# A hybrid trunk layer on one core: the state's decay applied as the state is taken, low-rank products in pairs, the inverse's blocks turned by VectorE, and the modulation blocks whole in the projection phase

## What is computed

```python
sh1, sc1, g1, sh2, sc2, g2 = split(silu(cond) @ ada_w + ada_b, 6)        # ada_w: 1024 x 6144
h = rms_norm(x) * (1 + sc1) + sh1
z = h @ w_in                                                             # 2816 columns
# half of the mixer: RWKV-7, two directions, 8 heads of 64, every step of time:
sa = state @ (-kk_t)
state = state * w_t + sa * b_t + v_t * k_t                               # w_t, b_t from low-rank products
y_t = state @ r_t
# other half: GLU, depthwise convolution of width 31, LayerNorm, swish
x = x + g1 * (concat(y_rwkv * gate, y_conv) @ w_out)
x = x + g2 * moe(rms_norm(x) * (1 + sc2) + sh2)                          # 32 experts, top 2 of a group
return rms_norm(x), last_states
```

## Time and profile before

| | us |
|---|---|
| median of 3 runs (lowest, highest) | 1218.47 (1215.95, 1225.31) |
| the profiled execution | 1215.16 |
| its span, first to last instruction | 1213.4 |
| PE, DVE, ACT, POOL busy in it | 988.4, 596.3, 301.8, 78.3 |
| mean granted TensorE clock | 0.812 of full speed |

### The profile page before, as it was taken

How to read it: one execution, slowest core, us unless ns; L and a number is a source line. 1 busy time by engine, 2 the same in 40 slices (tenths; PEclk the granted TensorE clock), 3 DMA queues, 4 the chain that set the end, 5 groups by cost and what they waited for, 6 DMA issues and landing times.

```text
span 1213.4 us, 16242 instructions
## 1 busy us (share of the span) xinstructions
PE 988.4 (81%) x6236; PEld 649.1 (53%) x6236; DVE 596.3 (49%) x1251; ACT 301.8 (25%) x542; POOL 78.3 (6%) x83
## 2 busy tenths in 40 slices
PE   1699899996988889899999869895289986889654
PEld 1367566764758768789799644453233332334121
DVE  2328947999686576667453244445711111111006
ACT  2240042222463434634121242111011111001002
POOL 0000000000110100010010000001111111010000
PEclk9989999997975775765565689896589998899777
DMA  9711221201313022124033528310689999799433
GB/s 314 256 35 52 74 63 48 66 18 40 106 27 88 18 49 66 36 73 111 1 97 72 203 105 284 150 52 35 243 326 414 421 419 421 300 418 421 190 146 128
DMA packets 77578, 193.81 MB, mean 160 GB/s; under 512 B 42501, under 2 KB 43071, under 8 KB 64831
## 3 DMA queue, kind: packets, MB, share of 16 engines
...
## 4 chain that ended last, share of the span: by engine, by line
PE 45%; DVE 15%; DMA 14%; ACT 4%; issue 3%; SPq 1%; DVEq 0%; POOLq 0%; ACTq 0%; POOL 0%
DMA arena<-in_expert_w_up 9%; PE bank L2138 7%; PE bank L1190 7%; PE bank L1550 4%; DVE arena L956 3%; PE bank L2160 3%; PE bank L1313 2%; PE bank L514 2%; PE bank L1240 2%; PE bank L1281 1%; PE bank L1227 1%; PE bank L1284 1%; PE bank L1252 1%; PE bank L1287 1%; DVE arena L1097 1%
## 5 line engine op out<-in xcount | busy, mean ns | idle before, releaser
L514 PE MATMUL bank<-arena 128*128 128x320 f32 x704 | 205.2, 447 | 6.3 <-DVE arena L416 4.1
L514 PEld LDWEIGHTS bank<-arena 128*128 128x128 f32 x704 | 134.1, 194 | 68.9 <-issue 19.3
L2138 PE MATMUL bank<-arena 128*64 128x512 f32 (+2 forms) x528 | 130.7, 658 | 34.6 <-DMA arena<-in_expert_w_up 33.7
L2138 PEld LDWEIGHTS bank<-arena 128*64 128x64 f32 (+2 forms) x528 | 46.1, 150 | 117.5 <-issue 116.2
L956 DVE SCALAR_TENSOR_TENSOR arena<-arena 128x655 f32<-128x655 f32 x116 | 104.7, 902 | 4.1
L1190 PE MATMUL bank<-arena 128*128 128x2 f32 x512 | 99.2, 324 | 6.3 <-DVE arena L1048 3.0
L1190 PEld LDWEIGHTS bank<-arena 128*128 128x128 f32 x512 | 97.1, 291 | 10.0 <-issue 7.2
L2218 DVE TENSOR_TENSOR arena<-arena,bank 128x256 f32<-128x256 f32 x17 | 7.2, 422 | 160.9 <-ACT arena L2192 160.9
L2160 PE MATMUL bank<-arena 128*64 128x512 f32 (+2 forms) x264 | 64.1, 627 | 10.0 <-DVE arena L2221 10.0
L1550 PE MATMUL bank<-arena 128*128 128x512 f32 x160 | 71.7, 606 | 0.0
L1550 PEld LDWEIGHTS bank<-arena 128*128 128x128 f32 x160 | 30.7, 194 | 37.7 <-issue 37.7
...
## 6 DMA issues: line engine op xcount, KB each, us to landing
arena<-in_expert_w_gate SPq DMA_DIRECT2D x33, 1024.0 KB, 15.1
...
arena<-in_ada_w SPq DMA_DIRECT2D x4, 2048.0 KB, 23.4
...
```

The costliest lines, as they stand in the source:

```text
L514: mm = nc.tensor.matmul(psum[4 + 2 * (n % 2) + half][:, 0:HALF], wring[:, n % NWIN, k], hT[:, k, half * HALF:(half + 1) * HALF], start=(k ...
L2138: mm = nc.tensor.matmul(psum[2 + n % 2][r, :], xeT[:, n % 2, c, r], gu[:, :, c, :], start=(c == 0), stop=(c == KD - 1))
```

## The change

- `ada_w` is given in tiles of 512 columns. Blocks 4 to 11 are computed as whole blocks like 0 to 3, in the projection phase, each followed by a join of another form: one product with the 128x2 selector as the stationary side gives a 2x512 row pair. VectorE adds the bias, GpSimd's queue stores the row pair. The 32 chunks, their loads, copies and the final turn go.
- The convolution's four pairs of tiles come first in `ZTILES`, before the gate.
- `scale` goes: BK is turned as it is, and the decay is applied in S on VectorE, (product x PC) + SP_, in two instructions of 64 columns in units 0 to 3 (two chunks a step), or a product and an addition of 512 columns in unit 4 (eight chunks a step).
- The low-rank products for decay and for learning rate of the same segment are issued next to each other; they use rows 0 to 63 and 64 to 127 of the array.
- `ta` is a 32x32 turn on VectorE, SBUF to SBUF, instead of 16 products and a ScalarE copy.
- The table of orders is written anew for all engines.

```diff
-        ZTILES = [("lora", 12), ("cb", 18), ("ca", 14), ("cb", 19), ("ca", 15), ("gate", 13), ("rkv", 0), ("rkv", 1),
-                  ("rkv", 4), ("rkv", 5), ("rkv", 8), ("rkv", 9), ("cb", 20), ("ca", 16), ("cb", 21), ("ca", 17),
+        ZTILES = [("lora", 12), ("cb", 18), ("ca", 14), ("cb", 19), ("ca", 15), ("cb", 20), ("ca", 16), ("cb", 21),
+                  ("ca", 17), ("gate", 13), ("rkv", 0), ("rkv", 1), ("rkv", 4), ("rkv", 5), ("rkv", 8), ("rkv", 9),
                   ("rkv", 2), ("rkv", 3), ("rkv", 6), ("rkv", 7), ("rkv", 10), ("rkv", 11)]
...
-            sp.dma_start(adaw[:, m % NADA].rearrange("p (a n) -> p a n", a=4),
-                         ins["ada_w"][4 * m:4 * m + 4].rearrange("a p n -> p a n")).then_inc(s_adaw[m % NADA], 16)
+            sp.dma_start(adaw[:, m % NADA], ins["ada_w"][m]).then_inc(s_adaw[m % NADA], 16)
+            if m >= 4:
+                if m == 4:
+                    sp.wait_ge(s_xT, TILES)
+                if m >= 6:
+                    sp.wait_ge(s_modblk, m - 5)
+                sp.dma_start(adab[0:2, m % 2],
+                             ins["ada_b"][0:1, m * 512:(m + 1) * 512].broadcast_to([2, 512])).then_inc(s_adab[m % 2], 16)
...
+        def mod_block(chain, m):
+
+            dve, i = nc.vector, m - 4
+            dve.wait_ge(s_modT, m + 1)
+            dve.wait_ge(s_adab[m % 2], 16 * (i // 2 + 1))
+            if i >= 2:
+                dve.wait_ge(s_modst[m % 2], 16 * (i // 2))
+            chain.announce(nc.vector.tensor_tensor(modblk[0:2, m % 2], psum[2][0:2, :], adab[0:2, m % 2], ALU.add),
+                           s_modblk, i + 1)
...
+        def pool_front():
+
+            for i in range(8):
+                nc.gpsimd.wait_ge(s_modblk, i + 1)
+                nc.gpsimd.dma_start(modrows[:, (4 + i) * 512:(5 + i) * 512], modblk[0:2, i % 2]
+                                    ).then_inc(s_modst[i % 2], 16)
...
-            w = adaw[:, m % NADA].rearrange("p (a k n) -> p k a n", a=4, k=KD)
+            w = adaw[:, m % NADA].rearrange("p (k n) -> p k n", k=KD)
             for k in range(KD):
                 g = 32 * (k % 4)
-                mm = nc.tensor.matmul(psum[m % 2][g:g + 32, :].rearrange("p (a n) -> p a n", a=4), condP[:, k, :],
-                                      w[:, k], start=(k < 4), stop=(k >= 4))
+                mm = nc.tensor.matmul(psum[m % 2][g:g + 32, :], condP[:, k, :], w[:, k, :], start=(k < 4), stop=(k >= 4))
             mm.then_inc(s_adamm, 1)
 
...
+            if m < 4:
+                for j in range(4):
+                    at = 256 + 2 * (4 * m + j)
+                    mm = nc.tensor.matmul(psum[3][:, at:at + 2], adatmp[:, m % 2, j * P:(j + 1) * P], const("sel"),
+                                          start=True, stop=True)
+            else:
+                if m > 4:
+                    pe.wait_ge(s_modblk, m - 4)
+                mm = nc.tensor.matmul(psum[2][0:2, :], const("sel"), adatmp[:, m % 2], start=True, stop=True)
             mm.then_inc(s_modT, 1)
...
+                elif ev == "adal":
+                    ada_load(u)
...
-                    sp.wait_ge(s_modst, 32)
...
+                    if u == 0 and m == 0:
+                        for stored in s_modst:
+                            act.wait_ge(stored, 64)
...
-                elif ev in ("ta0", "ta1"):
-                    for h in (int(ev[2]),):
-                        wait_filled(act, u, f"ta{h}")
-                        chain.announce(nc.scalar.activation(
-                            TA[0:32, 16 * h:16 * h + 16, :],
-                            psum[BANK[f"ta{h}"]][0:32, :].rearrange("p (n t) -> p n t", t=32), ACT.Copy),
-                            s_read[BANK[f"ta{h}"]], read_count(u, f"ta{h}"))
...
+                    if u == 0:
+                        dve.wait_ge(s_adamm, 12)
...
+                    if u:
+                        for q in range(4):
+                            wait_filled(dve, u - 1, f"t{q}")
...
+                elif ev in ("ta0", "ta1"):
+                    h = int(ev[2])
+                    dve.wait_ge(s_wcopy, 2 * u + 1)
+                    chain.announce(nc.vector.transpose(
+                        TA[0:32, 16 * h:16 * h + 16, :], GM[b][0:32, 16 * h:16 * h + 16, 0:32]),
+                        s_ta, 2 * u + h + 1)
...
-                    chain.announce(nc.vector.tensor_tensor(
-                        ST[:, (i + 1) % 2, 0:n], psum[5][:, 0:n * C].rearrange("p (n c) -> p n c", c=C), SP_[:, 0:n],
-                        ALU.add), s_ST, g + 2)
+                    new, summed = ST[:, (i + 1) % 2, 0:n], psum[5][:, 0:n * C].rearrange("p (n c) -> p n c", c=C)
+                    if n == 2:
+                        for k in range(n):
+                            at = i + k * steps(u)
+                            ins_ = nc.vector.scalar_tensor_tensor(new[:, k], summed[:, k], PC[b][:, at:at + 1],
+                                                                  SP_[:, k], ALU.mult, ALU.add)
+                            if k < n - 1:
+                                chain(ins_)
+                    else:
+                        pc = PC[b][:, i::steps(u)].unsqueeze(2).broadcast_to([P, n, C])
+                        chain(nc.vector.tensor_tensor(new, summed, pc, ALU.mult))
+                        ins_ = nc.vector.tensor_tensor(new, new, SP_[:, 0:n], ALU.add)
+                    chain.announce(ins_, s_ST, g + 2)
...
-                if ev == "scale":
-                    b = u % 2
-                    wait_filled(pool, u, "g7")
-                    pool.wait_ge(s_bk, u + 1)
-                    chain.announce(nc.gpsimd.tensor_tensor(BK, BK, PC[b].unsqueeze(2).broadcast_to([P, GC, 2 * C]),
-                                                           ALU.mult), s_bkh, u + 1)
...
-                if ev == "adac":
-                    pe.wait_ge(s_adac[u % 2], 16 * (u // 2 + 1))
-                    wait_free(pe, u, "ad")
-                    for k in range(KD):
-                        mm = nc.tensor.matmul(psum[BANK["ad"]][:, 0:2], adac[:, u % 2, k, :], condP[:, k, 0:2],
-                                              start=(k == 0), stop=(k == KD - 1))
-                    mm.then_inc(s_summed, 1)
...
-                elif ev in ("lora_w0", "lora_w1", "lora_a0", "lora_a1"):
+                elif ev in ("lora0", "lora1"):
                     pe.wait_ge(s_xl, 2)
                     pe.wait_ge(s_lora, 32)
                     if u == 0:
-                        pe.wait_ge(s_adatmp, 4)
+                        pe.wait_ge(s_modblk, 8)
                         pe.wait_ge(s_s0, 1)
-                    for name, r in ((("lw", slice(0, 64)),) if ev[5] == "w" else (("la", slice(64, 128)),)):
-                        for h, part in ((int(ev[6]), halves(u)[int(ev[6])]),):
-                            wait_free(pe, u, f"{name}{h}")
-                            for d, j, off, n, c0 in part:
-                                t0 = 0 if off == ZP else TP
-                                mm = nc.tensor.matmul(psum[BANK[f"{name}{h}"]][:, c0 % 512:c0 % 512 + n],
-                                                      lorab[r, d, j * P:(j + 1) * P], xlora[r, d, t0:t0 + n],
-                                                      start=True, stop=True)
-                            mm.then_inc(s_summed, 1)
+                    h = int(ev[4])
+                    part = halves(u)[h]
+                    for name in ("lw", "la"):
+                        wait_free(pe, u, f"{name}{h}")
+                    for s in part:
+                        d, j, off, n, c0 = s
+                        t0 = 0 if off == ZP else TP
+                        for name, r in (("lw", slice(0, 64)), ("la", slice(64, 128))):
+                            mm = nc.tensor.matmul(psum[BANK[f"{name}{h}"]][:, c0 % 512:c0 % 512 + n],
+                                                  lorab[r, d, j * P:(j + 1) * P], xlora[r, d, t0:t0 + n],
+                                                  start=True, stop=True)
+                            if s is part[-1]:
+                                mm.then_inc(s_summed, 1)
...
-                    pe.wait_ge(s_bkh if name == "t" else s_shiftD, (u + 1) * (1 if name == "t" else 3))
+                    pe.wait_ge(s_bk if name == "t" else s_shiftD, (u + 1) * (1 if name == "t" else 3))
...
-                                wait_read(pe, u, f"ta{h}")
+                                pe.wait_ge(s_ta, 2 * u + h + 1)
...
-            pool_mix(chain)
+            pool_front()
...
-    arrays["in_ada_w"] = _by_tile(arrays["in_ada_w"][0], 128)
+    arrays["in_ada_w"] = _by_tile(arrays["in_ada_w"][0], 512)
```

80 lines of the change are left out of this document (22 added, 58 removed), and 154 rows, old and new, of the table ORDER.

## The result

The changed kernel took 1176.4 us (median of 4 runs, 1172.5 to 1180.8), beside 1217.4 for the kernel before in the same rounds: ratio 0.965, 95% interval 0.960 to 0.971. The profiled execution has a span of 1170.8 us; before it was 1213.4. The stages, as windows of the trace after, in the columns of the earlier trace rows: the projection, units 0 to 3, their sum.

A forecast was written before the change was run, and what follows sets the result against it. TensorE's queue was taken to bound the scans. Scans -77.6, projection +13 and behind the scans -4 make -69 from 1215.2, so 1146.6; with 3.3 for the median, 1150 us, range 1120 to 1190.

The forecast's parts named there:

- What bounds the kernel: Scans: TensorE's queue bounds them; 22.4% of the chain there, 79 us, lies on L1190, the modulation chunks.
- The cap by VectorE: Scans, units 0 to 2: about 195 us of VectorE work at 85% busy gives 230 us.
- the two models: Scans: TensorE's path gives 269 us, VectorE's work plus the last unit by path gives 282; 277 was taken.
- The last unit: Unit 3 of the scans: too little VectorE work to be bound by it, so by the path 52 us.
- VectorE and the clock take more back: First rival, chance 0.24: scans take 305 us, TensorE idles more, its products run at 1.2 GHz; 1179 us in all.
- The turn: Scans: 32x32 turns leave TensorE's path, 14.5 us less; VectorE's turns add 5.5 us ahead of the merges.
- The S pair: Recurrence in the scans: S becomes two VectorE instructions, 0.25 us more in each of 32 steps, +8 us.
- GpSimd's hold: Scans: GpSimd's scaling held up VectorE's shift instructions; removing it gives back 6.0 us of VectorE on the chain.
- The projection: Projection: eight added blocks and joins, waits for VectorE's copies, less late-tap idle time; +13 us, ends +4 and +28.
- Behind the scans: After the scans: w_out loaded early, convolution's reload about 5 us instead of 8.76; -4 us, ends 0 and -5.
- Low-rank pairs: Paired low-rank products: some 8 us of TensorE's time but nothing of the scans' path; 0 to -8 for the range.
- The two new waits: VectorE's next BK waits for TensorE's last turn; TensorE's first low-rank product waits for the last block; nothing counted.

The follow-up runs named there:

- The doubled trip: Changed kernel with the inverse's diagonal blocks stored to memory twice in a row, the second after the first landed: 0.978 to the kernel before, 1193.4 us.
- three parts in the old order: Kernel before with modulation blocks in the projection, decay in S and turn by VectorE, its own tile order and table of orders, low-rank products unpaired: 0.980, 1194.9 us.
- The modulation alone: Kernel before with only eight whole modulation blocks in the projection and no chunks in the scans, all other orders as before: 0.986, 1197.0 us.
- grams first: Changed kernel with the next unit's chunk products and masks earlier, and ScalarE's last projection turn ahead of the shift: 0.961 to the kernel before, 1171.3 us.

## Why the prediction was right, and where it was not

The forecast was 1150 us in a range of 1120 to 1190; the time was 1176.4. The sign and the whole range held; the forecast's own range, 1130 to 1170, did not. Of the 69 us that the sum promised 42.6 came. The scans were 20 us longer than forecast (297.0 for 277) and the projection's cost 8.8 us higher; the front, which the sum left out, gave 2.4 back. So the time is where the forecast said only because the range took in the first rival.

- **What bounds the kernel** ("TensorE's queue bounds the scans"). Half right. The chain's 79 us for L1190 were taken as path. With that part alone 30.0 us came out, and 57.4 of 87.4 us of TensorE's work turned into idle time, most of it waits of the recurrence's steps, which the chunks had filled.
- **The cap by VectorE** (units 0 to 2 at 195 / 0.85 = 230 us) came out, 228.6, in part by luck: VectorE had 188.4 us of work there and not 195, and was busy 82% of the time and not 85%, two errors that cancel. And the term had the wrong reason: with the old table VectorE had 194.5 us of work in the three units, and they took 255.3 us. A busy share taken from one stretch is no bound that VectorE's amount of work sets. The forecast then took 277 us between the two models' 269 and 282, without a reason, which is 5 of the 20 us.
- **The last unit: "by the path, 77.6 less 25.3 for its chunks and 3.8 for turns, and plus 3 = 52".** This step failed, and it was the largest error in one place, 68.4 for 52: VectorE is busy 41.1 of 68.4 us there, and the unit is as long as gram, two trips through memory, inverse and merges of the next unit take one behind another. The doubled trip shows the first of the two trips on that path. Some 5.6 of the 16.4 us came with the new table, since the same unit took 62.8 us with three parts in the old order; the blocks are stored 16.5 us after its first step and not 10.5.
- **The rival "VectorE and the clock take more back"** had 1179 us and 305 in the scans, for 1176 and 297; its time was right, its mechanism only in part. VectorE did take more back. The clock did not: it rose from 0.62 to 0.67. But the reason given for the rise, that the chunks keep the clock low, holds for little of it: with the chunks alone gone it was 0.63, with three parts in the old order 0.65. In the changed kernel both levels stand in each unit, the high one mostly at its start and the low one in its later steps (two rows in the last section). So the rival's case, all products of the scans at 1.2 GHz, did not come true. It had been weighed by the Trainium skill's page TensorE: Matmul & The Clock Gate, section "Why this matters for your kernels", which asks to keep TensorE busy and warns of gaps. The scans neither bear that out nor refute it. Against it, have the low level over 20 us in which TensorE is never idle, and the changed kernel, whose longest gap there is 6.4 us for 3.3 before, has the higher mean clock. For it, TensorE is busy 75% of the time in the row at the high level and 59% in the one at the low level.
- **The turn** was sized at 14.5 - 5.5 us by busy and chain shares. Undoing it costs 22 us in the new order, and doing it gives nothing in the old. Its duration, 0.69 us a piece by the nearest row, was right (702 ns).
- **The S pair**: 8 us predicted; busy it is 28 x (0.57 - 0.29) = 7.8 us. The prediction had 32 steps at 0.25 us, but a unit's last step has no S: a count too high and a price too low. **GpSimd's hold**: 6.0 predicted, 5.9 shown for the shifts, some 2.4 more for two other lines.
- **The projection**: +13 predicted (4 to 28), +21.8 measured. Seven of the eight blocks took 1.93 us each, the last one 2.99. They landed 8.0 to 15.2 us after their issue. Three of them took over 13 us, which the prediction named as a sign that the forecast falls, but only the last one, at 9.6 us, made TensorE wait, 3.1 us; so that sign was badly set. The modulation alone, with the late taps of the old tile order, gives +18.5. So of the return that I counted for the early taps, the idle time before unit 0's first step, nothing shows. In its place TensorE waits 5.0 us at 307 us for ScalarE, which stands behind a copy that follows the inverse on VectorE, and 7.3 us for such copies. VectorE reached the copy of tile index 12 at 231.0 us (about 235 forecast).
- **Behind the scans**: -4 predicted, -4.4 measured; the reload of the convolution now lands 4.1 us after its issue (median of its four transfers; 7.0 in the kernel before), and the chain, where it had 8.76 us, no longer passes through it.
- **Low-rank pairs** at nothing: held, as far as the pairs of 128 columns go. The two new waits, put at nothing too, do not show among the waits of either engine.

What stays open: how the 26.7 us that the new table gives in units 0 to 2 divide among its single moves, how much of the turn's 22 us is its place in the order, and whether grams first is really faster than the changed kernel; 5 us are within what these runs can tell.
